# Second mixer of a two-block transformer kernel: projections in one stream, join, output gemm and norm by token tile

## The reference, cut to what matters

```python
(gq, gk, gv, gr, glr_f, glr_b, dq, dk, dv, dz, dab, m_a, m_b) = jnp.split(proj, points, axis=-1)
...
o_a = from_heads(rms_norm_2(o, gla_norm_w)) * jax.nn.silu(gr.astype(f32))
qkv = jax.nn.silu(centred_depthwise_conv(jnp.concatenate([dq, dk, dv], axis=-1), conv_w))
...
q = l2_norm(to_heads(cq, GDN_HEADS)) * (GDN_DK ** -0.5)
k = l2_norm(to_heads(ck, GDN_HEADS))
...
g_f = -jnp.exp(a_log_f.astype(f32))[None, :, None] * jax.nn.softplus(a_f + dt_bias_f.astype(f32)[None, :, None])
beta_f = jax.nn.sigmoid(b_f)
...
o_b = from_heads(rms_norm_2(o, gdn_norm_w)) * jax.nn.silu(dz.astype(f32))
mixed = jax.nn.sigmoid(m_a.astype(f32)) * o_a + jax.nn.sigmoid(m_b.astype(f32)) * o_b
return mixed.astype(h.dtype) @ w_out
...
x = x + token_mixer(h, w_in[i], ...)
h = rms_norm_2(x, norm2_w[i])
```

## Time and profile before

| | us |
|---|---|
| median of 3 runs | 5028.59 (5028.2 to 5028.96) |
| profiled execution | 5034.01 |
| its span in the trace | 5032.2 |
| mean granted TensorE clock | 0.846 |
| v and gr gemm, its first weight load to last copy | 2307.4 to 2493.9 |
| gemm of 3104 columns, working part | 2508.7 to 2783.7 |
| convolution stage, working part | 2810.1 to 3139.4 |
| norm preparation | 3411.7 to 3500.7 |
| join | 4030.8 to 4230.5 |
| output gemm and norm | 4230.5 to 4402.2 |

### The profile page before, as it was taken

How to read it: one execution, slowest core, us unless ns; L and a number is a source line. 1 busy time by engine, 2 the same in 40 slices (tenths; PEclk the granted TensorE clock), 3 DMA queues, 4 the chain that set the end, 5 groups by cost and what they waited for, 6 DMA issues and landing times. The chain is left out here.

```text
span 5032.2 us, 61951 instructions
## 1 busy us (share of the span) xinstructions
PE 3645.2 (72%) x24858; PEld 2864.2 (57%) x24858; DVE 1940.4 (39%) x2415; ACT 1048.3 (21%) x1574; POOL 900.6 (18%) x624
## 2 busy tenths in 40 slices
PE   3698785745759999737899788981699803559992
PEld 1698443745645555435799677651588802456661
DVE  4311545343136666324111355554345466211112
...
GB/s 247 82 103 77 6 11 100 76 138 98 74 231 79 63 63 15 76 147 116 88 76 76 80 90 40 67 128 208 119 118 110 77 179 92 171 159 357 332 272 184
DMA packets 355546, 606.89 MB, mean 121 GB/s; under 512 B 60319, under 2 KB 225055, under 8 KB 350849
## 3 DMA queue, kind: packets, MB, share of 16 engines
...
HBM read 433.67 MB, written 170.25 MB: 120 GB/s over the span
## 5 line engine op out<-in xcount | busy, mean ns | idle before, releaser
L455 PE MATMUL in_ps_p<-in_wh,h 128*128 128x352 f32 (+1 forms) x1600 | 363.3, 315 | 21.1 <-DVE in_wl L468 21.1
L455 PE MATMUL out_ps_p<-out_wh,m 128*128 128x256 f32 (+1 forms) x1152 | 277.8, 334 | 53.7 <-DVE out_wl L468 53.7
L455 PEld LDWEIGHTS in_ps_p<-in_wh,h 128*128 128x128 f32 x1600 | 273.6, 191 | 21.8 <-DVE in_wl L468 12.1
L455 PE MATMUL rest__ps_p<-rest__wh,h 128*128 128x388 f32 x1024 | 265.9, 341 | 15.5 <-DVE rest__wl L468 15.5
L1822 PE MATMUL cg_ps_p<-h,cg_wh 128*128 128x512 f32 x768 | 247.1, 404 | 14.3 <-POOL cg_wl L1801 14.3
L1594 PE MATMUL la_ps_s<-la_q,la_k 104*128 104x512 f32 x960 | 254.6, 401 | 2.5 <-DVE la_q L1674 2.5
L3217 PE MATMUL ex_ps_g<-ex_wgu,ex_xt 128*128 128x256 f32 x1024 | 234.4, 388 | 27.0 <-DVE ex_xt L3268 13.6
L455 PE MATMUL in_ps_p<-in_wl,h 128*128 128x352 f32 (+1 forms) x800 | 250.9, 314 | 0.0
L1632 ACT ACTIVATE la_pt<-la_ps_s 128x1024 f32<-128x1024 f32 x160 | 163.7, 1023 | 400.5 <-PE la_ps_s L1594 400.5
L455 PEld LDWEIGHTS out_ps_p<-out_wh,m 128*128 128x128 f32 x1152 | 199.4, 193 | 75.9 <-issue 46.0
L1549 POOL TENSOR_TENSOR la_accp<-la_accp,la_pt 128x1024 f32<-128x1024 f32 x80 | 195.1, 2438 | 229.6 <-ACT la_pt L1632 229.6
...
## 6 DMA issues: line engine op xcount, KB each, us to landing
...
ex_wgu<-in_moe_w_up_dram SPq DMA_DIRECT2D x32, 1024.0 KB, 11.3
...
```

Of the source, the lines that this page charges most:

```text
L455: mm = te.matmul(ps[n % NB][:, 0:cw], a, b, start=k == 0 and n_ == 0, stop=k == kt - 1 and n_ == 2)
```

## The change

Three things. First, mixer_gemm (mx) takes the place of gvr_, rest_ and cg: one unrolled stream of 16 chunks of 512 columns. Two are plain (v), six are convolution chunks (c, four units each), eight are gate chunks (g), each made of 256 columns of a sigmoid gate and the 256 of the silu gate that belongs to it. The norms of q and k are taken in the unit itself: ACT squares each 128x128 of the transposed tile with an accumulator, DVE adds epsilon, POOL takes the power, and ACT scales on the way out. A gate unit ends as sigmoid(m) * sigmoid(z) * z * norm weight, one tensor of 1024 columns per branch. Weights come in halves of 128x2048, split by DVE and POOL. Second, dp is gone; the table of decay and beta is computed in gt, whose low-rank projection takes dab as further rows of the same matmuls. Third, join_out (jo) takes the place of jm, out2 and n4: eight token tiles in a pipeline of two buffers each, in which TensorE goes G0 of tile t, transposes T of t+1, G1 of t, transposes H of t-1. Linear attention and delta rule read v2, c2, qk and gs instead of gvr, c2, qk and gs. In names, sa and sf are the squares of both branches, fb the sum of both directions, ea and pa epsilon and power, mx the products with norm and gate, ad the sum of branches, hi and lo the split, xs the residual sum, sx, ex, px its norm, hn the normed tile, ht the turned copy.

Its core in mixer_gemm (chunks, orders, and the steps that other engines wait for):

```diff
+    plain = [("v", [v_at + c * BANK], c) for c in range(D // BANK)]
+    wide = [("c", [c_at + c * BANK], c) for c in range(3 * D // BANK)]
+    gated = [("g", [g[0] + c * GW, g[1] + c * GW], (x, c)) for x, g in enumerate(gates) for c in range(D // GW)]
+    chunks = plain + wide + gated
...
+    pe_order, act_order, dve_order, pool_order = ["taps"], ["taps"], ["hi0_0", "lo0_0", "hi1_0", "lo1_0"], []
+    for n, (j, kind, i) in enumerate(units):
+        pe_order += [f"mm_{n}"] + ([f"tr_{n - 1}"] if n - 1 in cu else [])
+        act_order += ([f"sl_{n - 1}"] if n - 1 in cu else []) + [f"ev_{n}"] + ([f"ot_{n - 2}"] if n - 2 in cu else []) + ([f"sq_{n - 1}"] if normed(n - 1) else [])
+        dve_order += [f"c{t}_{n}" for t in range(3)] if kind == "c" else [f"rp_{n}"] if kind == "g" else []
+        dve_order += [f"ep_{n - 1}"] if normed(n - 1) else []
+        dve_order += [f"c{t}_{n}" for t in range(3, taps)] if kind == "c" else []
+        pool_order += ([f"pw_{n - 1}"] if normed(n - 1) else []) + ([f"g1_{n}", f"g2_{n}"] if kind == "g" else [])
+        if i in at_step(kind) and j + 1 < len(chunks):
+            q = at_step(kind).index(i)
+            dve_order += [f"hi{q}_{j + 1}"]
+            pool_order += [f"lo{q}_{j + 1}"]
...
+                        op = gp.tensor_tensor(wl[s][:, parts[q], :], wt[q][:], wh[s][:, parts[q], :].bitcast(F32), ALU.subtract)
+                    elif nm == "pw":
+                        t = ss[cu[n] % 2]
+                        gp.wait_ge(*dve.at(f"ep_{n}"))
+                        op = gp.tensor_tensor(t[:], t[:], half_c.to_broadcast([P, S // P]), ALU.pow)
+                    elif nm == "g1":
+                        e, r = eo[tu[n] % 4], sr[gu[n] % 2]
+                        gp.wait_ge(*dve.at(f"rp_{n}"))
+                        op = gp.tensor_tensor(e[:, 0:GW], e[:, 0:GW], r[:, GW:BANK], ALU.mult)
+                    else:
+                        e = eo[tu[n] % 4]
+                        x = chunks[units[n][0]][2][0]
...
+                        op = act.activation(sr[t % 2][:], ps[bank[n] // 2][:, bank[n] % 2, :], ACT.Sigmoid)
...
+                            op = act.activation(ot[c % 2][:, t, :], tp[c % 2][:, t, :], ACT.Square, accum_out=ss[c % 2][:, t:t + 1])
...
+                            act.wait_ge(*pool.at(f"pw_{n}"))
+                            for t in range(S // P):
+                                op = act.activation(ot[c % 2][:, t, :], tp[c % 2][:, t, :], ACT.Copy, scale=ss[c % 2][:, t:t + 1])
...
+                    elif nm == "rp":
+                        t = tu[n]
+                        ve.wait_ge(*act_s.at(f"ev_{n}"))
+                        if t >= 4:
+                            ve.wait_ge(e_out[t % 4], 16 * (t // 4))
+                        op = ve.tensor_tensor(eo[t % 4][:, 0:GW], ps[bank[n] // 2][:, bank[n] % 2, 0:GW], sr[gu[n] % 2][:, 0:GW], ALU.mult)
```

In gla_tables, the orders, and the load of the two sets of rows:

```diff
-    pe_order, act_order, dve_order = ["lr"], ["lr0", "lr1"], ["hl", "ll", "hq0", "lq0", "hk0", "lk0"]
+    D2, NT = 2 * DH, S // P
+    pe_order, act_order, dve_order = ["lr"], ["lr0", "lr1", "da0", "da1"], ["hl", "ll", "hq0", "lq0", "hk0", "lk0"]
     for u, (h, hf) in enumerate(units):
-        pe_order += [f"z0_{u}", f"z1_{u}", f"q_{u}"] + ([f"sc_{u - 1}", f"tr_{u - 1}"] if u else []) + [f"k_{u}"]
-        act_order += [f"{n}{d}_{u}" for n in ("az", "ex", "ln", "e1", "de", "e2") for d in both] + ([f"s0_{u - 1}", f"s1_{u - 1}", f"kl_{u - 1}"] if u else [])
-        dve_order += [f"{n}{d}_{u}" for n in ("la", "cu", "qd") for d in both] + \
+        pe_order += [f"z0_{u}", f"z1_{u}", f"q_{u}"] + ([f"sc_{u - 1}", f"tr_{u - 1}"] if u else ["dab"]) + [f"k_{u}"]
...
+        dve_order += [f"{n}{d}_{u}" for n in ("la", "cu", "qd") for d in both] + (["gmax", "gsum", "neg", "one", "g", "rec"] if u == 1 else []) + \
             ([f"{n}{'qk'[hf]}{h + 1}" for n in "hl"] if h + 1 < GH else []) + ([f"{n}_{u - 1}" for n in ("ma", "mb", "ad")] if u else []) + \
-            [f"{n}{d}_{u}" for d in both for n in ("ki", "kt")]
+            [f"{n}{d}_{u}" for d in both for n in ("ki", "kt")] + (["gadd"] if u == 0 else [])
...
+                for j, src in enumerate((w_lr, w_dab)):
+                    sp.dma_start(wr[:, :, j * R2:(j + 1) * R2], src.rearrange("(k p) n -> p k n", p=P)).then_inc(wr_in, 16)
```

In join_out:

```diff
+    NT, HK, NH = S // P, KT // 2, GH + DH
+    both = range(2)
+    parts = [slice(0, HK), slice(HK, KT)]
+    pieces = [(c, q) for c in both for q in both]
+    ok = lambda t: 0 <= t < NT
+    pe_order, act_order, dve_order, pool_order = ["T_0"], [], [], []
+    act_order += ["wh_0", "wh_1", "sa_0", "sf_0", "hi_0", "wh_2", "wh_3", "sa_1", "sf_1"]
+    dve_order += ["wl_0", "wl_1", "ea_0", "mx_0", "ad_0", "lo_0", "wl_2", "wl_3", "ea_1", "mx_1", "ad_1"]
+    pool_order += ["fb_0", "pa_0", "fb_1", "pa_1", "fb_2"]
+    for t in range(NT + 2):
+        for o, names in ((pe_order, (("G0", t), ("T", t + 1), ("G1", t), ("H", t - 1))),
+                         (act_order, (("sx", t - 1), ("sa", t + 2), ("sf", t + 2), ("hi", t + 1), ("ht", t - 2))),
+                         (dve_order, (("xs", t - 1), ("ex", t - 1), ("ea", t + 2), ("lo", t + 1), ("hn", t - 1), ("mx", t + 2), ("ad", t + 2))),
+                         (pool_order, (("px", t - 1), ("pa", t + 2), ("fb", t + 3)))):
+            o += [f"{nm}_{i}" for nm, i in names if ok(i)]
...
+                        act.wait_ge(*pool.at(f"fb_{t}"))
+                        if t:
+                            act.wait_ge(*act_s.at(f"sf_{t - 1}"))
+                        for h in range(DH):
+                            op = act.activation(jf[:, h * P:(h + 1) * P], f[s][:, h * P:(h + 1) * P], ACT.Square, accum_out=ss[s][:, GH + h:GH + h + 1])
...
+                        ve.wait_ge(*pool.at(f"pa_{t}"))
+                        ve.wait_ge(g2_in[s], 32 * (t // 2 + 1))
+                        for h in range(GH):
+                            at = slice(h * GV, (h + 1) * GV)
+                            ve.scalar_tensor_tensor(a[s][:, at], a[s][:, at], ss[s][:, h:h + 1], ga[s][:, at], ALU.mult, ALU.mult)
+                        for h in range(DH):
+                            at = slice(h * P, (h + 1) * P)
+                            op = ve.scalar_tensor_tensor(f[s][:, at], f[s][:, at], ss[s][:, GH + h:GH + h + 1], gb[s][:, at], ALU.mult, ALU.mult)
+                        op.then_inc(*dve.did(o))
+                    elif nm == "ad":
...
+                    elif nm == "xs":
+                        ve.wait_ge(*pe.at(f"G1_{t}"))
+                        ve.wait_ge(x_in_s[s], 16 * (t // 2 + 1))
+                        ve.tensor_tensor(xt[s][:], py[s][:].rearrange("p c n -> p (c n)"), xt[s][:], ALU.add).then_inc(*dve.did(o))
```

And where they are called:

```diff
-            gemm_stage(nc, "gvr_", h[:, :, :, :], lat, w2[:, GV:LR], gvr, 512)
-            gemm_stage(nc, "rest_", h[:, :, :, :], lat, w2[:, DZ:], rest, (w2.shape[1] - DZ) // 8)
-            conv_gemm(nc, ident, h[:, :, :, :], w2[:, CV:DZ], gdn_conv_w_2[0], c2)
+            mixer_gemm(nc, ident, half, h[:, :, :, :], w2, D, CV, [(2 * D, DZ + D + 32), (DZ, DZ + 2 * D + 32)], gdn_conv_w_2[0],
+                       [gla_norm_w_2[0], gdn_norm_w_2[0]], v2, qk, c2, gates)
...
-        gdn_prep(nc, c2, rest[:, D:D + 32], [gdn_a_log_fwd_2[0], gdn_a_log_bwd_2[0]], [gdn_dt_bias_fwd_2[0], gdn_dt_bias_bwd_2[0]],
-                 half, qk, gs)
...
-        with nc.sbuf_tensor("m2", [P, 2, KT, S], F32) as m:
-            join_mix(nc, ident, gla, gdn, [gvr[:, D:2 * D], rest[:, 0:D]], [rest[:, D + 32:2 * D + 32], rest[:, 2 * D + 32:]],
-                     gla_norm_w_2[0], gdn_norm_w_2[0], half, m[:, :, :, :])
-            gemm_stage(nc, "out2", m[:, :, :, :], lat, w_out_2[0], y2, 512)
         with nc.sbuf_tensor("h3t", [P, KT, S], F32) as h:
-            norm_stage(nc, "n4", ident, S, x3, norm2_w_2[0], y=y2, x_out=x4, h_t=h[:, :, :], h_out=h3)
+            join_out(nc, ident, half, gla, gdn, gates, w_out_2[0], x3, norm2_w_2[0], x4, h3, h[:, :, :])
```

More of the change, by code:

```diff
@@ new lines, in mixer_gemm @@
+    U = len(units)
+    first = [n for n, (j, kind, i) in enumerate(units) if i == 0]
+    final = [n - 1 for n in first[1:]] + [U - 1]
+    conv = [n for n in range(U) if units[n][1] == "c"]
+    toks = [n for n in range(U) if units[n][1] != "c"]
+    cu, tu = {n: k for k, n in enumerate(conv)}, {n: k for k, n in enumerate(toks)}
+    gts = [n for n in range(U) if units[n][1] == "g"]
+    gu = {n: k for k, n in enumerate(gts)}
+    normed = lambda n: n in cu and cu[n] < NQK
+    at_step = lambda kind: (0, 1) if kind == "c" else (1, 3)
@@ L2041, in _ @@
                     act.activation(lr_t[0:R2, hf * HB:(hf + 1) * HB], pz[hf][0:R2, :], ACT.Copy).then_inc(*act_s.did(f"lr{hf}"))
+                for hf in both:
+                    act.activation(da_t[:, hf * HB:(hf + 1) * HB], pz[hf][R2:2 * R2, :], ACT.Copy).then_inc(*act_s.did(f"da{hf}"))
                 def give(u):
@@ new lines, in _ @@
+                weight(0)
+                sums(0)
+                weight(1)
```

(14 more changed lines are left out.)

747 lines of the change are left out of this document (407 added, 340 removed).

## The result

The changed kernel takes 4646.22 us (median of 4 runs, 4641.77 to 4655.78) against 5028.77 of the kernel before: a ratio of 0.9239, 95% interval 0.9222 to 0.9255, so 382.6 us less. The forecast was 4672, 356.6 less than the 5028.59 that it started from; the measured time lies inside its range.

What follows compares the result with a forecast made beforehand. Bounds seen: seams between stages, two stages without TensorE, and their 1.2 GHz clock. 5034.0 - 102.3 - 89.0 + 5 - 169.4 = 4678.3, in terms of the median 4672.9, stated as 4672; range 4632 to 4725.

Steps and rivals of the forecast that it cites:

- Projections, -102.3: From first weight load to table stage: 847.3 us before, 745.0 forecast, with 80 plain or gate and 24 convolution units.
- The seams: Breaks between stages ended by barriers; two added back were predicted to cost +28 to +36 us in the projections.
- the ring inside a normed unit: Chain of ACT and DVE steps in a normed convolution unit, forecast at 11.2 us, just fitting TensorE's 11.78.
- Rival 2: Projections: a normed convolution unit outlasts TensorE's 11.78 us, +32 us, whole kernel 4705; chance 14%.
- Norm preparation, -89.0: Separate stage of 89.0 us, forecast to disappear because its norms move into the convolution units.
- Table stage, +5: Stage that takes over the decay table: 0 if hidden, about 10 if all on the path, +5 taken.
- Join, -169.4: Join with the gemm and norm behind it: 371.4 us before, 202 forecast as a pipeline of eight token tiles.
- 20.4 us per tile: Join: alternating ACT and DVE steps, 18.3 us with latencies, plus 2.1 for one meeting of DVE with POOL.
- the collision: Join: a DVE pass slowed while POOL adds two operands, once per tile, +2.1 us.
- the filling: Start of the join until its pipeline runs, forecast at 68 us: 32 for the first tile, then 12 and 12.
- TensorE cold in the join: Rival: clock drops between bursts in the join, so a tile takes 24.4 us; +24, whole kernel 4697; chance 18%.
- Rival 3: Join: DVE and POOL do not collide and the pipeline starts sooner, -22 to -35 us, whole kernel 4642; chance 10%.

## Why the prediction was right, and where it was off

**Projections, -102.3 against -106.5.** Right in its parts. The 80 plain and gate units and 24 convolution units at warm pace are the stretch: TensorE is busy for 724.2 of 740.75. The first matmul of the gemm came 12.2 us into the stretch (11.3 forecast), and 5.0 lay behind the last one (7 forecast). The "4 to 5 in the convolution units" were 1.9. The seams came at 15.7 each, within the 14 to 18 expected. What was off is the size of the ring inside a normed unit: 11.2 us forecast, 9.0 measured. Its steps and their order were right; the squares took 2.26 us and not 3.5, the small DVE step 0.08 and not 0.3, and the 0.5 of latencies is inside the other steps. The squares were priced at 0.43 apart from the earlier trace rows, where line L1158 waits before each square for the one before it (act.wait_ge(sqs, i)); those of the change have no such wait and start 0.25 apart. That the wait makes the difference is my reading of the code, no run tests it. Rival 2 (+32) rested on this ring and did not happen; squares three times show that it would have needed 3 us more per unit.

**Norm preparation, -89.0.** Right, and the removal costs nothing elsewhere, as the run without norms shows.

**Table stage, +5 against +8.0.** Inside the bounds of 0 and 10.

**Join, -169.4 against -198.2.** The mechanism was right and the size off, mainly in the term of 20.4 us per tile. Between the residual sums of tiles 0 and 4 a turn takes 16.7. It breaks down like this: the twelve squares cost 4.0 (0.40 and 0.295 apart), not 5.7; the square of the residual with its store's issue 1.1, not 1.6, since the issue runs beside it (the store is issued at 3918.12, the square starts at 3918.11); the products with the collision 5.9, not 6.8; and 0.4 of latencies is inside the other steps. The squares are off for the same reason as above. The first residual sum came 59.4 us into the join against 68, and from the first to the last of them it took 102.8 against 122 (the last three steps were 14.6, 9.8 and 11.8). 9 + 19 + 1 at the end make the 29. The measured join lies below the forecast's own lower bound of about 180, since that bound kept the squares' price.

Two slips in the forecast's count partly hid each other. The parts that it names for the filling add up to 56 us (32, 12 and 12), not 68; and it has six steps behind the filling (five turns and the last gemm halves), where seven lie between the first residual sum and the last. With the filling as itemised and the missing turn its own prices give 56 + 6 x 20.4 + 32 = 210, so 202 was 8 us nearer to the measured 173 than they deserved, and that is luck. The itemised 56 is also close to the 59.4 measured.

**Rivals.** TensorE cold in the join (18%) did not happen: the three tiles had 0.80, 1.00 and 0.90, and the pace of 16.7 was ACT's and DVE's; but the run with one tile after another shows 0.64 with waits of 6.7 and 12.7 us in each tile. Rival 3 (4642, 10%) is the nearest in the whole time, 4 us off, while 4646 lies just outside the 4672 +/- 25 to which the forecast gave 53%. Its shorter filling happened (59.4 against the 68 of the forecast); its other half did not: the collision was there, 2.1 us a tile as priced, and what made the ring shorter was the squares.
